# Moving columns and PSUM columns of the plain projection products taken from last to first

## The reference, cut to what matters

```python
q, v, f_fw, f_bw, g = jnp.split(h @ w_in, HG_SPLITS, axis=-1)        # layer 0, x and ctx
y = (o * jax.nn.silu(g)) @ w_out
z, xbc, dt_raw = jnp.split(h @ w_in, [MB_INNER, MB_INNER + MB_CONV_CH], axis=-1)   # layer 1
a, v = jnp.split(h @ w_up, 2, axis=-1)                               # both layers
y = (jax.nn.silu(conv(a)) * v) @ w_down
```

## Time and profile before

| | us |
|---|---|
| median of 3 runs | 1389.62 (1389.42 to 1391.38) |
| span of the profiled execution | 1389.7 |
| TensorE busy in it | 1321.6 (95%) |
| VectorE busy | 894.5 (64%) |
| ScalarE busy | 647.9 (47%) |
| GpSimd busy | 332.2 (24%) |

### The profile page before, as it was taken

The page is one execution under the profiler, slowest core; times in us unless marked ns, Lnnn a source line. Parts: engine busy times, 40 slices in busy tenths (PEclk is TensorE's granted clock), DMA queues, the critical chain, the costliest instruction groups (busy, mean ns, idle before and its releaser), DMA issues.

```text
span 1389.7 us, 21292 instructions
## 1 busy us (share of the span) xinstructions
PE 1321.6 (95%) x7893; PEld 1116.2 (80%) x7893; DVE 894.5 (64%) x1706; ACT 647.9 (47%) x1023; POOL 332.2 (24%) x227
## 2 busy tenths in 40 slices
PE   5999999999998999999999989999999988899997
PEld 2678888888765888888888757888888877899997
DVE  4567776677687644323455778777777857665573
ACT  4435445444355433223333266555555645654554
POOL 1000000000202654105551030211111301780961
PEclk9999999999999999999999999999999999999999
DMA  9634333325461632334324424433333465456643
GB/s 346 180 128 130 122 124 125 125 88 193 152 212 31 182 99 68 91 106 121 91 68 137 121 91 122 152 91 91 91 93 95 132 203 161 122 166 179 201 135 107
DMA packets 274788, 183.16 MB, mean 132 GB/s; under 512 B 6643, under 2 KB 249107, under 8 KB 274707
## 3 DMA queue, kind: packets, MB, share of 16 engines
q1 hardware_dynamic: 274162, 180.00, 42.8%
q10 hardware_dynamic: 544, 2.10, 0.4%
HBM read 181.03 MB, written 1.05 MB: 131 GB/s over the span
## 4 chain that ended last, share of the span: by engine, by line
PE 80%; DVE 12%; ACT 5%; issue 2%; DMA 1%; POOL 1%; DVEq 0%; ACTq 0%
PE bank L2135 20%; PE bank L2137 20%; PE bank L2136 20%; DVE wl L1341 3%; PE bank L2150 2%; PE bank L2151 2%; PE bank L2152 1%; ACT wh L820 1%; PE bank L2201 1%; DVE conv L1800 1%; PE bank L2721 1%; PE bank L2250 1%; PE bank L2708 1%; PE bank L2707 1%; PE bank L2709 1%
## 5 line engine op out<-in xcount | busy, mean ns | idle before, releaser
L2135 PE MATMUL bank<-hh,wh 128*128 128x512 f32 (+1 forms) x1298 | 461.0, 355 | 10.8 <-DVE wl L1341 5.1
L2137 PE MATMUL bank<-hh,wl 128*128 128x512 f32 (+1 forms) x1298 | 456.4, 352 | 0.0
L2136 PE MATMUL bank<-hl,wh 128*128 128x512 f32 (+1 forms) x1298 | 455.8, 351 | 0.0
L820 ACT ACTIVATE wh<-wraw 128x1024 fp32r<-128x1024 f32 (+2 forms) x265 | 256.4, 985 | 108.4 <-PE bank L2137 97.2
L1341 DVE TENSOR_TENSOR wl<-wraw,wh 128x1024 fp32r<-128x1024 f32 (+2 forms) x187 | 205.7, 1122 | 136.3 <-ACT wh L820 136.3
L2135 PEld LDWEIGHTS bank<-hh,wh 128*128 128x128 f32 x1298 | 247.4, 191 | 45.7 <-DVE wl L1341 7.5
L2137 PEld LDWEIGHTS bank<-hh,wl 128*128 128x128 f32 x1298 | 247.2, 190 | 32.6
L2136 PEld LDWEIGHTS bank<-hl,wh 128*128 128x128 f32 x1298 | 247.6, 191 | 30.3
L1800 DVE SCALAR_TENSOR_TENSOR conv<-bank,pv,conv 128x189 f32<-128x189 f32 (+3 forms) x396 | 173.1, 437 | 131.9 <-ACT conv L1093 103.6
L711 POOL TENSOR_TENSOR wl<-wraw,wh 128x1024 fp32r<-128x1024 f32 x78 | 186.9, 2407 | 174.3 <-ACT wh L820 173.9
L2135 PE MATMUL bank<-fh,wh 128*128 128x512 f32 (+1 forms) x352 | 120.1, 341 | 2.9 <-POOL fl L731 2.7
(11 more groups left out here) (338 smaller groups left out, 1928.8 us busy)
## 6 DMA issues: line engine op xcount, KB each, us to landing
wraw<-in_ffn_w_up SPq DMA_DIRECT2D x88, 512.0 KB, 3.8
araw<-in_ada_w SPq DMA_DIRECT2D x40, 1024.0 KB, 7.3
wraw<-in_mb_w_in SPq DMA_DIRECT2D x48, 512.0 KB, 4.0
wraw<-in_hg_w_in SPq DMA_DIRECT2D x40, 512.0 KB, 3.8
wraw<-in_ffn_w_down SPq DMA_DIRECT2D x32, 512.0 KB, 3.9
wraw<-in_mb_w_out SPq DMA_DIRECT2D x16, 512.0 KB, 4.5
gates<-in_ada_w SPq DMA_DIRECT2D x5, 1024.0 KB, 9.4
wraw<-in_hg_w_out SPq DMA_DIRECT2D x8, 512.0 KB, 4.8
```

The source lines that it names most:

```text
L820: act.activation(wh[:, n % SLOTS, 0:size], wraw[:, n % SLOTS, 0:size], ACT.Copy).then_inc(w_hi, 1)
L2135: pe.matmul(dst, W, hi(k), start=(k == 0), stop=False, **skip)
L2136: pe.matmul(dst, W, lo(k), start=False, stop=False, **skip)
L2137: ins = pe.matmul(dst, L, hi(k), start=False, stop=(k == nk - 1), **skip)
```

## The change: what it does

In `gemm` the PSUM destination and both moving operands are reversed along their columns. A matmul's first column is then the tile's last one, read from the highest address, and its result is written to the last column of the destination; each further step goes one column back. Every result lands where it did before. The weights, the number and order of instructions, and the waits stay as they are.

```diff
         def gemm(dst, w, hi, lo, nk, k0=0, need=None):
 
             skip = dict(skip_group_check=True) if k0 else {}
+            back = dst[:, ::-1]
             for k in range(k0, nk):
                 if need is not None:
                     need(k)
-                W, L = w(wh, k), w(wl, k)
-                pe.matmul(dst, W, hi(k), start=(k == 0), stop=False, **skip)
-                pe.matmul(dst, W, lo(k), start=False, stop=False, **skip)
-                ins = pe.matmul(dst, L, hi(k), start=False, stop=(k == nk - 1), **skip)
+                W, L, H = w(wh, k), w(wl, k), hi(k)[:, ::-1]
+                pe.matmul(back, W, H, start=(k == 0), stop=False, **skip)
+                pe.matmul(back, W, lo(k)[:, ::-1], start=False, stop=False, **skip)
+                ins = pe.matmul(back, L, H, start=False, stop=(k == nk - 1), **skip)
             return ins
```

## The result

The changed kernel takes 1403.27 us, the median of 4 runs (1401.12 to 1403.34), against 1389.58 us (1389.42 to 1391.38) for the kernel before: a ratio of 1.0094, 95% interval 1.0080 to 1.0109. It is slower by 13.7 us. The forecast was 1389.6 us; the rival named B, "the address term grows", had a price of 1405.7.

What follows compares the result with a forecast made beforehand. The prediction took TensorE, busy 95% of the 1389.7 us span, and gemm's three matmul lines (830 us of the path) as the bound; its terms summed 0 + 0 + 0 + 0 to a forecast of 1389.6 us, range 1345 to 1430 us.

Steps and rivals of the forecast that it cites:

- Rival B: gemm's moving reads: backward reading meets the weight load more often, hh at 512 goes as fh, +16.1 us, 1405.7; chance 0.22.
- What bounds the kernel: TensorE: busy 95% of the 1389.7 us span, with gemm's three matmul lines owning 60% of the path, 830 us.
- Step 1: Instructions on all queues: nothing added or removed, same 4950 matmuls, weight loads, waits and order; cost in instructions none.
- Step 2: gemm's moving read and PSUM write, last to first: taken as 0, with bounds of 216.6 to 430 ns at 512 columns.
- Rival A: gemm's read or write: every pair of columns is lost, two clocks a column, +791 us, 2181 us; chance 0.17.
- Step 3: gemm's address-dependent term on each matmul: taken as 0, with tile bounds from -6.7 to +17.3 us.
- Step 4: Handover from an ascending to a descending matmul in the same bank, eight products: taken as 0, at worst 1.3 us.
- Step 5: PSUM readers need the whole bank, so see no difference; nearly all of a TensorE gain or loss reaches the end.
- Rival C: gemm's matmuls: the address term shrinks, to a floor of -53 us, 1337 us, or half of it, 1363; chance 0.19.
- Rival D: gemm's two reversals are folded away as both sides turn together; 1389.6 us, within the forecast's chance.
- same: Whole kernel: time within 0.2% (2.8 us) of before, 0.56 ns for each of 4950 matmuls; chance 0.42.

Runs made afterwards that it cites:

- the shifted one: The kernel before, all products forward, with an unused 32-byte tile behind hl so weights and later tiles lie 32 bytes on: 1402.12 us against 1390.83, ratio 1.0084.

## Why the prediction failed, by its steps

**What bounds the kernel** held: the three lines of gemm own the path, and the distances, which give 11.8 to 13.6 us, account for the 10.5 to 13.7 measured. Three remarks beside the steps were wrong: that nothing lies around the span (each run is 1.7 to 1.8 us longer than its own span, the profiled one of the kernel before too); that the excess is nearly the same at 256 and at 512, which fh, with 11.1 and 20.0, contradicts; and that 0.56 ns is within one clock, which is 0.42 ns.

**Step 1** (no instruction added) held: 21292 instructions in both, the same counts by group.

**Step 2** (no pair of columns lost; 0, bounds up to 430 ns) held. The distance at 512 rose by 3%, not to double. Rival A, 2181 us, is dead, and with it the strict reading of the Trainium skill's rule in "PSUM — Partial Sum Buffer", Specifications (TRN2), that any non-contiguous pattern slows matmuls significantly: with the write alone turned the distance stays 226.7 ns and the time 1.0001 of before.

**Step 3** (the address-dependent term) is the step that failed, by the prediction's own test: hh at 512 between 216 and 237 ns and other than 227, with the z rows as before. (What the runs tie to the backward read as such, a growth with the width, touches the subject of step 2 too, which took the backward read for free.) It was taken as 0, within tile bounds of +16.1 us for hh at 512 and -3.2 for hh at 256. What was measured lies at or near these ends: +6.6 x 2442 = +16.1 and -1.7 x 1452 = -2.5, with near 0 for both of fh (over all distances rather +14.5, -2.4 and -0.3). The ground for taking 0, that an excess of 13.3 ns at 256 and at 512 alike "looks like a cost for each matmul and not for a direction", took a state for a law. The equal 13.3 was found only level with the weights; fh, with 20.0 ns at 512 and 11.1 at 256, showed in the same table that the excess can grow with the width, and it was read as a curiosity of its address. It was the ordinary case (28.9 ns for 64 columns), and hh the exception. A row that sits at a good value for an unknown reason has only that value to lose when what it rests on is moved.

**Step 4** (handover into the same bank) held: no cost shows. Other products mostly lie between the two parts, so single handovers can't be read; but the 75 distances from any other matmul to one of gemm sum to 15.1 us before and 14.5 after, where its upper bound would have added 1.3.

**Step 5** held: the waits of the earlier trace rows moved by about 1 us, and the profiled span grew by 9.7 us for a sum of distances of 11.8, of which 0.91 would be 10.7.

**Rival B** had the size, 1405.7 us, the sign and the row to look at, and was given 0.22. The time also lies inside the stated range; what failed is the forecast of no change. The ground of B was only half right. It spoke of the lines of the moving read meeting the weight load; but a weight load of a quarter the length, and standing weights, leave the backward read at 233.3 ns. The weights matter for the forward read: reading 512 different columns, 226.7 ns was seen only with a full load and level addresses. The Trainium skill, "TensorE: Matmul & The Clock Gate", Part 2, step 1, says that the two operands have independent read ports and the load steals nothing. The backward rows agree with it (233.3 ns with 128 and with 32 weight columns); the forward ones don't, since 32 bytes between the operands' addresses change 226.7 to 233.3 ns. **Rival C**, a gain, is what the 256-column products from hh did: 1.7 ns each. **Rival D**, that the two reversals are folded away, is out: the distance changed, and the read alone and both together give the same 233.3 ns.

The forecast's chance for "same", 0.42, needed the average to hold within 0.56 ns, and rested on no row that showed a backward read at that rate; the chances on step 3 alone should have been split by the two tile states that the rows showed, 227 or 233, as all else was excluded.

What stays open: what in the memory or in TensorE's read path the lost step is, why the time grows as by one in thirteen, and what about the history sets the value. That the changed kernel and the shifted one are slow for the same reason rests on equal distances and on costs that don't add, not on a look inside. That repeating 64 bytes costs more (242 ns) than running on, repeating 16 bytes nothing, and that 256 bytes are the period, points to a memory laid out in turns of 16 to 256 bytes, but that is argued, not shown.

## What to carry to other kernels

This was measured for float32r products with a weight load for each matmul. Measure such a stream by the distance of starts, by tile and by width, and compare with columns over clock. Where two tiles of the same shape differ by some ns, look at where they start against the weights: 32 unused bytes cost 11 us here. Keep 512-column moving tiles forward and level with the weights modulo 256 bytes, and don't assume that what is best at 512 columns is best at 256.

## What the runs showed of the hardware that was not expected

- A backward PSUM write costs nothing measurable (1.0001, 0.9991 to 1.0010), nor does a backward moving read in plain fp32 (215.8 ns a record both ways at 256 columns). In float32r it takes 28.9 ns for 64 columns, level with the weights, and at 512 columns 233.3 ns at fourteen of fifteen other addresses.
- The distance of float32r matmuls at 512 columns depends on the two operands' addresses, with a period of 256 bytes: 226.6 ns when level, 228.9 with 64 bytes between, mostly 231 to 235 elsewhere (and 233.4 when both lie 16 bytes on).
- The same stretch can have more than one settled speed (113.2 or 117.8 ns at 256 columns, 64 bytes off), by what ran before.
- A shorter weight load can make a matmul stream slower: 226.7 ns with 128 weight columns, 5.56 / 24 = 231.7 with 32, at 512 columns; at 256 it makes it faster (120.0 to 113.3).
